# Moving one weight split, one factor difference and the copies of turned probabilities in a hybrid mLSTM and attention layer

## The reference, cut to what matters

```
h    = rms_norm(x) * (1 + scale) + shift
proj = h @ w_in                      # split into xa va oa za ia fa qa ka vat zb ga gb
xc   = silu(conv(xa))
y_m  = (head_norm(sigmoid(oa) * mlstm(xc @ w_q, xc @ w_k, va, ia, fa)) + skip * xc) * silu(za) @ w_out_mlstm
o_a  = sum over 3 groups of softmax(lse) * dilated_window_attention(rotary(qa), rotary(ka), vat)
y_a  = (o_a * silu(zb)) @ w_out_attn
out  = rms_norm(x + gate * ((sigmoid(ga) * y_m + sigmoid(gb) * y_a) @ w_out))
```

## Time and profile before

| | |
|---|---|
| median of 3 runs | 1365.64 us (1365.32 to 1367.71) |
| the profiled execution | 1365.64 us, span 1363.8 us |
| mean granted clock of TensorE | 0.997 |
| busy in the span: PE, DVE, ACT, POOL | 98%, 67%, 44%, 35% |
| a head of `mix` | 119.8 us from one head's end to the next |

### The profile page before, as it was taken

How to read it: one execution, slowest core, us unless ns; L and a number is a source line. 1 busy time by engine, 2 the same in 40 slices (tenths; PEclk the granted TensorE clock), 3 DMA queues, 4 the chain that set the end, 5 groups by cost and what they waited for, 6 DMA issues and landing times. The chain is left out here.

```text
span 1363.8 us, 17501 instructions
## 1 busy us (share of the span) xinstructions
PE 1337.2 (98%) x6405; PEld 1120.5 (82%) x6405; DVE 913.7 (67%) x1511; ACT 594.6 (44%) x1039; POOL 481.9 (35%) x308
## 2 busy tenths in 40 slices
PE   8999999999999999999999999999999998999998
PEld 6888888888888888888888888888888886888786
DVE  7988766573744445535368856866876689669676
ACT  7663353344444344333545455354545543233122
POOL 0097555454554555542101200210120024542541
PEclk9999999999999999999999999999999999999999
DMA  9522323322234334327232741553272162246332
GB/s 333 182 80 96 131 102 124 124 93 104 112 124 139 124 127 151 139 108 216 84 90 63 217 93 32 167 144 94 63 209 70 33 217 77 93 136 231 112 93 93
DMA packets 63759, 171.22 MB, mean 126 GB/s; under 512 B 21809, under 2 KB 21937, under 8 KB 62390
## 3 DMA queue, kind: packets, MB, share of 16 engines
q1 hardware_dynamic: 60794, 162.44, 36.1%
q10 hardware_dynamic: 2880, 7.65, 1.9%
HBM read 127.38 MB, written 41.65 MB: 124 GB/s over the span
## 5 line engine op out<-in xcount | busy, mean ns | idle before, releaser
L1275 POOL TENSOR_TENSOR wlo<-wraw,whi 128x1024 fp32r<-128x1024 f32 x28 | 74.5, 2661 | 430.3 <-ACT whi L1495 406.1
L739 POOL TENSOR_TENSOR wlo<-w_sum,whi 128x512 fp32r<-128x512 f32 x112 | 164.8, 1473 | 137.2 <-ACT whi L864 137.2
L616 PE MATMUL banks<-t_hi,wlo 128*128 128x512 f32 x448 | 174.3, 389 | 0.0
L614 PE MATMUL banks<-t_hi,whi 128*128 128x512 f32 x448 | 174.3, 389 | 0.0
L615 PE MATMUL banks<-t_lo,whi 128*128 128x512 f32 x448 | 174.3, 389 | 0.0
L1010 DVE TENSOR_TENSOR c_sum<-c_sum,banks 128x512 f32<-128x512 f32 x196 | 134.4, 686 | 46.0 <-PE banks L616 32.0
L614 PE MATMUL banks<-h_hi,whi 128*128 128x512 f32 x416 | 162.1, 390 | 0.7 <-POOL wlo L1275 0.7
L616 PE MATMUL banks<-h_hi,wlo 128*128 128x512 f32 x416 | 161.9, 389 | 0.0
L615 PE MATMUL banks<-h_lo,whi 128*128 128x512 f32 x416 | 161.9, 389 | 0.0
L864 ACT ACTIVATE whi<-w_sum 128x512 fp32r<-128x512 f32 x112 | 70.5, 630 | 165.8 <-PE banks L616 100.7
L614 PE MATMUL banks<-whi,h_hi 128*128 128x512 f32 x256 | 99.9, 390 | 0.0
(11 more groups left out here) (410 smaller groups left out, 2975.2 us busy)
## 6 DMA issues: line engine op xcount, KB each, us to landing
wraw<-in_w_all SPq DMA_DIRECT2D x68, 512.0 KB, 4.4
raw<-in_w_all SPq DMA_DIRECT2D x28, 512.0 KB, 4.4
queries_keys<-fin SPq DMA_DIRECT2D x12, 1024.0 KB, 4.0
qa<-queries_keys SPq DMA_DIRECT2D x12, 768.0 KB, 11.9
s_wada<-in_w_ada_cols SPq DMA_DIRECT2D x16, 512.0 KB, 6.0
attn_values<-fin SPq DMA_DIRECT2D x6, 1024.0 KB, 4.0
tn<-attn_values SPq DMA_DIRECT2D x12, 512.0 KB, 9.1
merge_gates<-fin SPq DMA_DIRECT2D x5, 1024.0 KB, 3.9
```

Source lines behind the costliest of these rows:

```text
L614: t_.matmul(out, w_hi, x_hi, start=first, stop=False)
L616: return t_.matmul(out, w_lo, x_hi, start=False, stop=last)
L739: nc.gpsimd.tensor_tensor(wlo4[:, o % 4, :], source(r, j), whi4[:, o % 4, :].bitcast(F32), subtract).then_inc(s_split, 1)
L1275: nc.gpsimd.tensor_tensor(to, wraw[:, q % 2, :], hi.bitcast(F32), ALU.subtract).then_inc(w_split, 1)
```

## The change

Three edits.

1. ACT instead of DVE copies the turned probabilities `pT` from PSUM in each of the 12 steps of a head in which there are some, after its copy of `num` and ahead of the exponentials of the step.
2. ACT makes the high part of the next head's chunk 0 at point 20 (`TURN - 3`), ahead of the two sigmoids of point 21, instead of at point 11. POOL's subtraction follows it.
3. In `merge` the fourth factor difference, `difference(7)`, goes on DVE ahead of `low(2)`, and its high part `sum_high(7)` on ACT ahead of the loop over the products.

```diff
@@ mix, scalar
+                if 1 <= x <= 4:
+                    act.wait_ge(p_turned, i * 12 + 4 * g + x)
+                    bs = [blocks_of(g, 2 * (x - 1) + u) for u in range(2)]
+                    bank = A1.rearrange("p (u b q) -> p u b q", u=2, b=2)
+                    if bs[0] == bs[1]:
+                        ins = A(pT[:, :, 0:bs[0], :], bank[:, :, 0:bs[0], :], ACT.Copy)
+                    else:
+                        for u in range(2):
+                            ins = A(pT[:, u, 0:bs[u], :], bank[:, u, 0:bs[u], :], ACT.Copy)
+                    ins.then_inc(p_kept, 1)
...
-                            if h:
+                            if h and n > ZA:
                                 next_high(n + 2)
...
                         mixing(u)
+                        if u == TURN - 3:
+                            next_high(ZA + 2)
                         if u == TURN - 2:
                             z_sigmoid(ZA)
                             z_sigmoid(ZB)
@@ mix, vector
-                if 1 <= x <= 4:
-                    dve.wait_ge(p_turned, i * 12 + 4 * g + x)
...
-                        ins = v.tensor_copy(pT[:, :, 0:bs[0], :], bank[:, :, 0:bs[0], :])
...
-                            ins = v.tensor_copy(pT[:, u, 0:bs[u], :], bank[:, u, 0:bs[u], :])
-                    ins.then_inc(p_kept, 1)
@@ merge, scalar
         sum_high(4)
+        sum_high(7)
         for o in range(TOTAL, WITH_BRANCH):
...
-            if o == TOTAL:
-                sum_high(7)
@@ merge, vector
         difference(4, low_left[0], bt_raw[6], 6)
+        difference(7, low_right[0], up_right)
         low(2, low_left[0])
         low(4, bt_raw[4])
         low(6, bt_raw[6])
-        difference(7, low_right[0], up_right)
         low(7, bt_raw[7])
```

More of the change, by code:

```diff
@@ L1789, in attend @@
                     v.tensor_scalar(nm[:, x % 2, :], st[:, g, 2 * x:2 * x + 2, 0], -1.0, None, ALU.mult).then_inc(max_done, 1)
-                if 1 <= x <= 4:
-                    dve.wait_ge(p_turned, i * 12 + 4 * g + x)
-                    bs = [blocks_of(g, 2 * (x - 1) + u) for u in range(2)]
-                    bank = A1.rearrange("p (u b q) -> p u b q", u=2, b=2)
-                    if bs[0] == bs[1]:
-                        ins = v.tensor_copy(pT[:, :, 0:bs[0], :], bank[:, :, 0:bs[0], :])
-                    else:
-                        for u in range(2):
-                            ins = v.tensor_copy(pT[:, u, 0:bs[u], :], bank[:, u, 0:bs[u], :])
-                    ins.then_inc(p_kept, 1)
             def weigh_groups(j):
```

## The result

| | before | after |
|---|---|---|
| median | 1365.68 us (1365.32 to 1367.71, 4 runs) | 1381.97 us (1380.80 to 1382.11, 4 runs) |
| ratio to before | | 1.0115, 95% interval 1.0103 to 1.0128 |
| profiled execution, span | 1365.64 us, 1363.8 us | 1380.80 us, 1379.0 us |
| mean granted clock | 0.997 | 0.991 |

The change makes the kernel 16.3 us slower by the medians; the forecast was +10.3 us (1376, range 1369 to 1381). The sign was right, the size was 6 us short, and the median lies 1 us outside the range. Runs of one kernel lie up to some 4 us apart (those of before from 1363.96 us at a mean clock of 0.997 to 1368.42 at 0.995), so a gap of 1 or 2 us between two medians tells little.

A forecast was written before the change was run, and what follows sets the result against it. PE, busy 98% of the span, bounds the kernel, so only its waits cost time. Point 12 -5.2, heads 0 to 2 +13.05, head 3 and `merge` +2.4 (-5.3 + 7.7): +10.3 us on 1365.64, 1376 us, range 1369 to 1381.

The forecast's parts named there:

- The pauses at point 12, -5.2 us: Point 12 of each head: PE's 1.29 us wait for `pT` goes, four times, -5.2 us.
- Both together remove the 1.29 us: Point 12: ACT's copies and the moved chunk split jointly remove PE's 1.29 us idle time in each head.
- edit 1 alone would bring little: Point 12: with only ACT's copies, the exponential still hangs on the same delayed DVE, so little is gained.
- Heads 0 to 2, +13.05 us: Ends of three heads: bank 1 freed 3.25 us late and chunk 3's subtraction 1.1 us late, 3 x 4.35 us.
- 4.35 us a head: Heads 0 to 2: loss in each, 3.25 us for bank 1 plus 1.1 us for chunk 3.
- Head 3: End of head 3: `szb` issued at 1094.15, PE starts behind bank 1 at 1100.75 instead of 1093.39, 7.4 to 10.3 us late.
- `ct`, +7.7 us: Start of `merge`: the load of `ct`, first on DVE's list, is issued 7.7 us later, behind the next weight split.
- `next_high(7)` (1.0) and POOL (2.4) behind 1100.7 bring it to 1104.5: Ahead of `merge`: ACT's high part and POOL's subtraction follow `keep(5, 1)`, moving `ct` from 1096.82 to 1104.5, +7.7 us.
- Edit 3, -5.3 us: In `merge`: with the difference ahead of the low parts, product 3 starts at 1158.1 instead of 1162.88; with clock, -5.3 us.
- do 4, 6 and 7 from 1149.9 on without a pause: In `merge`: after waiting 3.1 us for product 2, PE runs these products back to back, reaching product 3 at 1158.1.
- Alone it may lose some of this to the clock: In `merge`: without the other edits, the early difference may lose part of its 5.3 us gain to the clock.
- the delays of the convolution grow: Rival, three heads: group weights, fold's low part and `ew` late, 1379 to 1382 us; with a late ACT, chance 0.17.

The follow-up runs named there:

- edit 2 alone: Only the moved split of the next head's first chunk, to point 20, against the kernel before; 1382.59 us, ratio 1.0119.
- the version without edit 1: The whole change with the split at point 12 instead of 20 and the `pT` copies left on DVE; 1356.91 us, ratio 0.9940 to before.
- with `szb` ahead of the load: The changed kernel with the load of `szb` ahead of the weight load at SP's place 5, statistics saves still behind; 1372.59 us, ratio 1.0049 to before.
- PE busy in the pause: Edit 3 on the kernel before, plus 24 identity transpositions on PE ahead of product 2's wait; 1362.28 us, ratio 0.9973 to before.
- split at point 12: All three edits, with the moved chunk split at point 12 instead of 20; 1357.85 us, ratio 0.9940 to before.
- With the saves ahead: The changed kernel with `szb` and the statistics' six writes ahead of the weight load at SP's place 5; 1367.72 us, ratio 1.0011 to before.
- four places: All three edits with the chunk split at point 12 (1357.85 us), 15 (1362.12), 18 (1376.52) or 20, the change itself (1381.97).
- edit 3 alone: Only the early `difference(7)` and `sum_high(7)` in `merge`, against the kernel before; 1363.02 us, ratio 0.9974.
- the split at point 18: All three edits, with the moved chunk split at point 18 instead of 20; 1376.52 us, ratio 1.0091 to before.

## Why the prediction was right in sign and short in size

Two terms were too favourable, and both lie behind head 3: the delay of `ct` was put at 7.7 us and measured 10.6, and the gain of edit 3 was put at 5.3 us and measured 2.7. The rest of the sum held, in part by luck.

**The pauses at point 12, -5.2 us: about right in size, wrong in cause.** The 5.1 us of waiting for `pT` at point 12 are gone. The waits of the other attention steps, most of them at the heads' ends, fell from 2.2 us (`ew` 1.8, `sm` 0.4) to 1.2 (`pT` 0.8, `sm` 0.4) besides, which edit 1 brought (edit 2 alone still has the 1.8 for `ew`). "Both together remove the 1.29 us" does not hold: edit 2 alone and the version without edit 1 have no wait for `pT` either. That edit 1 alone would bring little held.

**Heads 0 to 2, +13.05 us: right in sum, by luck in the parts.** `og` of heads 0 to 3 starts at 729.08, 853.52, 975.73 and 1097.62 after, and at 730.74, 850.52, 970.31 and 1090.12 before. So the three head changes lost 4.7, 2.4 and 2.1 us net; with the 1.29 us gained in each head that is 6.0, 3.7 and 3.4, together 13.1 where I had 13.05 (13.7 with the 1.5 us a head by which the waits above fell). In the first of them PE waited 2.14 us for `og` and 1.34 for `keep`, and ran at the lower clock for 3.4 us (about 1.7 us, worked out from that), which I had foreseen only for `merge`. In the others it waited 2.13 and 0.74, then 2.14 and 0.45. Chunk 3 cost 0.4 us a head where I had 1.1. What is left, another 0.4 us a head, is in no wait of the list. My 4.35 us a head was too much for two heads and too little for the one with the lower clock, and these misses happened to cancel. The experiments show the mechanism: with `szb` ahead of the load the wait for `keep` goes, and with POOL away from `og` that wait goes.

**Head 3: right.** I had `szb` issued at 1094.15 and PE starting at 1100.75 in the frame of before. With the 7.5 us by which head 3 starts later that is 1101.65 and 1108.25; the trace has 1101.49 and 1107.89.

**`ct`, +7.7 us: this term was mis-sized, it measured 10.6.** DVE's first instruction with `ct` came 18.08 us later, and 7.50 of that is the heads. The step that failed is "`next_high(7)` (1.0) and POOL (2.4) behind 1100.7 bring it to 1104.5". I followed the load ahead of `ct` and left out the semaphore that `ct` waits for as well, the saves of the statistics. These stand behind the same late load, the last of them took 9.51 us, and `ct` was issued at 1114.07 where my step gives 1112.0 (1104.5 plus the heads' 7.5); the load itself was in time, at 1111.17. Its landing took 10.39 us instead of 9.6, which makes the rest. That the saves are a cause was shown by moving them, 4.9 us in the kernel that had `szb` ahead already.

**Edit 3, -5.3 us: also mis-sized, it measured -2.7 in the changed kernel and -3.6 alone.** From the start of `difference(4)` to product 3 it was 26.23 us before, from this row to the last of the earlier trace rows:

```profile
1136.65 3.38 DVE L2235 TENSOR_TENSOR bt_lo_raw<-um_lo_raw,bt_lo_raw 128x2048 f32<-128x2048 f32 x1
```

It is 1178.71 - 1154.70 = 24.01 after: 2.2 us less, and 0.5 more because product 3 is at the full clock at once (2.72 us instead of 3.21). The failed step is that PE would "do 4, 6 and 7 from 1149.9 on without a pause". I ended the list of DVE at `low(6)` and left out `low(7)`, one instruction of 3.3 us further, for which product 7 waits. Where product 2 is at the full clock (PE busy in the pause, split at point 12) the distance is 22.8 to 22.9, 1.4 us more than my 21.45. The other 1.2 us is the lower clock: in the changed kernel it holds for all 12 matmuls of product 2 (5.26 us instead of 2.73), more than DVE's pace hides. With the saves ahead it is 23.9, again with the whole of product 2 at the lower clock. So "Alone it may lose some of this to the clock" had it the wrong way round: alone, the clock cost nothing.

Added up: 10.3 predicted, -0.35 for the heads (7.5 instead of 7.85), +2.9 for `ct`, +2.6 for edit 3, is 15.45 us, and the spans differ by 15.2. Both misses went the same way, and the rival "the delays of the convolution grow", which had the next higher time, was not what happened: PE has no wait for the fold or for `ew`, and chunk 3 came out shorter.

The medians differ by 1.1 us more than the profiled spans because the profiled execution of after is the shortest of its four runs (1380.80; the others are 1381.89 to 1382.11). What the other three did in that time is not known.

## What to carry to other kernels

Before a subtraction on POOL is moved, list what DVE has beside the new place, tiny instructions with two SBUF inputs included, and who waits for them; here four places cost nothing, 4 us, 19 us and 24 us. Then go through everything that stands behind the wait in the queue of transfers, and for each transfer through all the semaphores it waits for: the small saves of the statistics cost 4.9 us here beside the gate load's 9.4. Where a late factor is moved forward, follow the engine that makes the factors to the last one that the stretch needs, since it sets the end and not the consumer's pace.

## What the runs showed of the hardware that was not expected

An instruction of 8 elements a partition on DVE took 2.39 us beside a subtraction of POOL, and two of 128x1024 with a single tensor input took 3.52 us together instead of 1.54. But an instruction on one element, beside the subtraction at point 12, took only 0.58 us instead of 0.22: it started at 1067.22, and the subtraction ended at 1067.79.

A pause of PE of the same length did not always lower the clock. Ahead of product 2 it was 3.08 us with edit 3 alone and also with the split at point 12; in the first the window behind it is at 0.50, in the second at 1.00:

```profile
1142.00:1144.00 2.00, 0.98 (x4) 0.86 (x5) 2.00 (x2) 2.00 (x4) 1.87 (x2) 1.00 0.00 0
1144.00:1146.00 2.00, 2.00 (x9) 1.31 (x7) 2.00 (x1) 0.86 (x1) 2.00 (x2) 1.00 0.00 0
```

These are two windows of the kernel with the split at point 12, where product 2 starts at 1143.02. In the changed kernel a wait of 2.14 us for `og` was followed by the lower clock in head 0 and not in heads 1 and 2, whose waits are as long; with `szb` ahead it was head 2, with the split at point 18 heads 0 and 2, with edit 2 alone none of the three. A forecast can give such a term only a chance.

A save of the statistics, a few KB, took 9.51 us to be done in the changed kernel, with 371 GB/s on the DMA engines in the window 1103 to 1105 of the same trace, and 15.80 us with `szb` ahead of the load.
